# RWKV-7 chunks on one NeuronCore: the level products of two pairs of heads move to the crossed corners of the TensorE array, and the low-rank inputs of the factors are loaded a stage earlier

## The chip, the cores and the metric

The kernel runs on one core of one Trainium2 chip. The metric is the device time of one execution in microseconds (us), and less is better. A span or a start time in a profile counts from the first instruction of the profiled execution. TensorE is written PE, its weight loads PEld, VectorE DVE, ScalarE ACT, GpSimd POOL and SyncE SP.

## The reference, cut to what matters

One inference step of a hybrid layer: RWKV-7 time mixing and indexer-selected sparse attention side by side, merged by gates and followed by a gated convolutional FFN, for a prompt of 1024 + 16 tokens and 8 sample sequences of 8 tokens. Two parts of it matter here.

The first is how the RWKV inputs are prepared (`pm` holds the shifted projection, cut into r, k, v of 512 columns and three low-rank parts wd, ad, gd of 64, 64 and 128):

```python
w = -softplus(-(w0 + tanh(wd) @ w_w2)) - 0.5
decay = exp(-exp(w))
a = sigmoid(a0 + ad @ w_a2)
g = sigmoid(gd) @ w_g2
```

The second is the recurrence over tokens, for 8 heads with a 64 x 64 state each:

```python
def _rwkv7_step(S, inp):
    r, dec, k, v, kk, a = inp
    sa = einsum('bhvk,bhk->bhv', S, -kk)
    S = S * dec[..., None, :] + sa[..., None] * (kk * a)[..., None, :] + v[..., None] * k[..., None, :]
    return S, einsum('bhvk,bhk->bhv', S, r)
```

All values are fp32.

## The kernel before, in words

`program` runs stages one after another, each a block with a barrier behind it: normalisation and the attention projections, prompt attention with the remaining projections (`prompt_and_project`, it writes the 14 row tiles of the RWKV projection to `PM_dram`), the indexer scores of the samples (`sample_scores`, from L753), the RWKV factors (`rwkv_factors`, from L933), the RWKV chunks (`rwkv_chunks`, from L1136) and a `tail` with the rest. Every engine runs its own list in the order in which the code writes it; `wait_ge` on semaphores joins them. No planner reorders anything in these three stages.

**sample_scores.** POOL gathers 8 sequences of cached index keys into `KX` (L806, two buffers, the next gather waits until the buffer has been woven). ACT weaves two sequences into one tile (L818, semaphore `woven`), PE transposes them (L857), multiplies them with the queries (`dots`, L871), ACT rectifies (L830) and PE weighs them (L883). `dots` already uses four positions of the array: a product whose operands lie in partitions 0 to 63 or 64 to 127 writes its result to partitions 0 to 63 or 64 to 127, and all four combinations occur. Its moving operand is read with a step of 128 elements. SP writes scores to DRAM (L783 to L796) and waits for them at the end (L799).

**rwkv_factors.** SP issues 14 loads in this order: `PML` (the low-rank rows), `wa2` (two halves) and four vectors of `vec`, the k rows, two more parts of `vec`, then `g2`, `hsum`, `hback`, `keep`, `ones`, and last the r and v rows. ACT takes the tanh and the sigmoid of `PML` (L1037, L1038). PE and DVE wait for ten small loads (`small_in`, L990 and L1091) before they do anything. Then PE multiplies `PML` with `wa2` in 12 pieces (L997), ACT applies a sigmoid with a bias from `vec` (L1044), and DVE runs a scan with `keep` (L1098). ACT squares k (L1048), PE sums the squares (L1002), and 12 pieces of products and DVE work follow.

**rwkv_chunks.** 17 chunks of 64 tokens (the 17th with 16) and one chunk with the samples, 18 passes. Per chunk and head a unit lower triangular 64 x 64 matrix is inverted by levels of block doubling: 5 levels for a prompt chunk, 2 for the samples, 87 in all. Heads lie in pairs: pair p has one head in partitions 0 to 63 and one in 64 to 127. A level has these steps for all 8 heads:

- `level_q` on PE: Q = M Z into a PSUM bank A (8 matmuls, semaphore `q_done`), and right behind it the transpose of Z by a product with the identity into a bank B (8 matmuls, `t_done`).
- DVE masks Q out of bank A (L1503, `q_read`), and ACT copies the transpose out of bank B (L1432, `t_read`).
- `level_z` on PE: a product of the two into bank A (8 matmuls, `z_done`), and DVE adds it to Z (L1508, `z_ready`).

All three use `each`, whose matmuls have their operands and their result in the same half of the partitions:

```python
def each(out, lhsT, rhs, n=CH, at=0, step=CH):
    for p in range(4):
        for g in HEADS:
            o = at + step * p
            last = pe.matmul(out[g, o:o + n], lhsT(g, p), rhs(g, p), start=True, stop=True)
    return last
```

The order on PE is written out by hand. One pass c works on three chunks at once: the chain of chunk c (`chain_w`, `chain_u`, `chain_y`, `chain_s`, which carry the state), levels 2 to 4 of chunk c + 1, and the products (`gram_b`, `gram_t`, `gram_k`, `rows_bk`) and levels 0 and 1 of chunk c + 2. In full: chain_w(c), level_q(c+1, 2), gram_b, gram_t, chain_u, level_z(c+1, 2), gram_k, level_q(c+2, 0), chain_y, level_q(c+1, 3), chain_s, level_z(c+2, 0), level_z(c+1, 3), level_q(c+2, 1), level_q(c+1, 4), rows_bk, level_z(c+2, 1), level_z(c+1, 4). DVE does the two operations of the next state (L1514, L1516) between the mask of level 3 and the addition of level 0 of chunk c + 2. All matmuls of `each` are told apart in the profile by their tiles, not by their line: they are all L1233. An fp32 matmul stands in the trace as two records.

Of the kernel before, what the change touches and what calls it, by code (L numbers as in the profile page):

```python
# [4 lines left out]
F32 = mybir.dt.float32  # L5
I32 = mybir.dt.int32
U32 = mybir.dt.uint32
ALU = mybir.AluOpType
# [9 lines left out]
R = TP + TS  # L18
# [734 lines left out]
def sample_scores(nc, I, E, SC, ident):  # L753

    NR = 4 * 4
    with ExitStack() as sc:
        sc.enter_context(nc.cleanup_on_exit())
        def sb(name, shape, dt=F32):
# [14 lines left out]
                 "own_dotted", "own_rectified", "own_weighted", "own_placed", "own_sent")  # L773
        (woven, turned, evacuated, dotted, rectified, weighted, placed, ready,
         own_dotted, own_rectified, own_weighted, own_placed, own_sent) = (nc.alloc_semaphore(name=f"ss_{n}") for n in names)
        kx_in = [nc.alloc_semaphore(name=f"ss_kx_in{i}") for i in range(2)]
        sent = [nc.alloc_semaphore(name=f"ss_sent{i}") for i in range(2)]
        with nc.Block() as block:
            @block.sync
            def _(sp):  # L780
                sp.wait_ge(own_placed, 1)
# [30 lines left out]
            def _(act):  # L812
# [13 lines left out]
                for c in range(4 * NR):  # L826
# [4 lines left out]
                    if c % 16 == 7 and c // 16 < 2:  # L831
                        weave(c // 16 + 2)

# [98 lines left out]

def rwkv_factors(nc, I, PM_dram, PM, PML, F, PL):  # L933

    PARTS = [(0, 384), (384, 384), (768, 336)]
# [3 lines left out]
    with ExitStack() as sc:  # L939
# [3 lines left out]
        vec = sb("vec", [128, 7, 4])  # L943
        minus = sb("minus", [128, 4])
        wa2 = sb("wa2", [128, 512])
# [11 lines left out]
        names = ("small_in", "low_in", "k_in", "r_in", "v_in", "squashed", "squared", "sq_done", "bounded", "rooted",  # L957
                 "inverted", "w_done", "a_done", "g_done", "back_done", "bonus_done", "w_read", "a_read", "g_read",
                 "summed", "mapped", "normed", "bonused", "exps", "bonus_read")
        (small_in, low_in, k_in, r_in, v_in, squashed, squared, sq_done, bounded, rooted, inverted, w_done, a_done,  # L960
# [4 lines left out]
        with nc.Block() as block:  # L965
            @block.sync
            def _(sp):
                rows = PM_dram.rearrange("t p n -> p t n")
                sp.dma_start(PML[:, :, :], rows[:, 12:14]).then_inc(low_in, 16)
                for dst, src in ((wa2[0:64, :], I["w_w2"]), (wa2[64:128, :], I["w_a2"]),  # L970
                                 (vec[:, 0:4, :], I["rvec"][:, 0:4, :])):
                    sp.dma_start(dst, src).then_inc(small_in, 16)
                sp.dma_start(PM[:, 4:8], rows[:, 4:8]).then_inc(k_in, 16)
                for dst, src in ((vec[:, 5, :], I["rvec"][:, 4, :]), (vec[:, 6, :], I["lnb"]), (g2[:, :], I["w_g2"]),
                                 (hsum[:, :, :], I["hsum32"]), (hback[:, :, :], I["hback32"]),
                                 (keep[:, :], I["keep"]), (ones[:, :], I["ones_pair"])):
                    sp.dma_start(dst, src).then_inc(small_in, 16)
# [4 lines left out]
            def _(pe):  # L982
# [47 lines left out]
            def _(act):  # L1030
# [5 lines left out]
                act.wait_ge(low_in, 16)  # L1036
# [1554 lines left out]
```

## Time and profile before

| what | us |
|---|---|
| median of 3 timed runs (lowest, highest) | 3077.9 (3074.35, 3082.34) |
| the profiled execution's own time | 3106.72 |
| its span | 3104.9 |
| PE busy | 2777.5 (89%) |
| DVE busy | 1519.4 (49%) |
| ACT busy | 858.6 (28%) |

The three stages that the diff touches run one after another from 987 us of the span on. In a timeline a line holds the start, the length, the engine, the line of the code, the operation and its tiles, the number of records and, in brackets, the idle time ahead of it with what ended it. The times of matmuls in the trace overlap, because a matmul starts long before the one ahead of it has ended: a mean of 218 ns is the way of one through the array, and the distance between starts is what counts for throughput.

### The profile page before, as it was taken

Reading aid. Unit: us, or ns where it says so; the run is one execution under the profiler, and the core shown is the slowest. Engines: PE = TensorE matmul, PEld = TensorE weight load, DVE = VectorE, ACT = ScalarE, POOL = GpSimd, SP = SyncE. Lnnn points to the kernel's source line nnn. Section 1 sums busy time; section 2 is a strip of 40 time slices with the busy share of each in tenths; the row PEclk is TensorE's granted clock in tenths of the full one; section 3 lists DMA queues with packets and bytes.
Section 4 is the critical chain, followed back from the end, with each engine's and each line's share of the span. In section 5 each row is a group of like instructions: output and inputs, shape, how many; then the busy total and the mean of one; then the engine's idle time right before and its main releaser. Section 6 shows DMA issues by size and latency. Waiting matters only on the chain. (4 is left out here: it accounts for less than half of the span.)

```text
span 3104.9 us, 45137 instructions
## 1 busy us (share of the span) xinstructions
PE 2777.5 (89%) x17974; PEld 1725.7 (56%) x17974; DVE 1519.4 (49%) x2761; ACT 858.6 (28%) x1893; POOL 257.0 (8%) x291
## 2 busy tenths in 40 slices
PE   5897999998985968799869999979879999999998
PEld 3553466655653322799815566645546666556665
DVE  2001788894433426444356999998713320221111
ACT  1111522103533535222111233001235540134411
POOL 1000011000000000000000122000144410000000
PEclk9998999998996976899869999989889999999999
DMA  4001021231102440000016333225256643433332
GB/s 149 10 10 42 8 78 64 85 84 33 39 26 108 141 135 0 26 4 4 5 47 198 109 102 135 84 89 162 90 166 196 190 133 102 139 133 109 109 107 78
DMA packets 83041, 274.00 MB, mean 88 GB/s; under 512 B 17944, under 2 KB 39544, under 8 KB 70864
## 3 DMA queue, kind: packets, MB, share of 16 engines
q1 hardware_dynamic: 71056, 220.05, 21.6%
q0 software_dynamic: 11776, 51.07, 5.3%
q8 instruction: 142, 2.33, 0.3%
q14 instruction: 67, 0.55, 0.1%
HBM read 238.20 MB, written 32.16 MB: 87 GB/s over the span
## 5 line engine op out<-in xcount | busy, mean ns | idle before, releaser
L1885 PE MATMUL tl_P<-tl_XN,tl_WU 128*128 128x368 f32 x2112 | 670.9, 478 | 14.7 <-issue 8.6
L1885 PEld LDWEIGHTS tl_P<-tl_XN,tl_WU 128*128 128x128 f32 x2112 | 403.4, 192 | 269.5 <-issue 28.7
L346 PE MATMUL dp_PS<-xT,dp_W 128*128 128x368 f32 x1440 | 456.1, 474 | 0.0
L346 PEld LDWEIGHTS dp_PS<-xT,dp_W 128*128 128x128 f32 x1440 | 271.0, 191 | 163.0 <-issue 4.1
L1897 PE MATMUL tl_P<-tl_HT,tl_WD 128*128 128x368 f32 x1056 | 329.1, 473 | 0.0
L1897 PEld LDWEIGHTS tl_P<-tl_HT,tl_WD 128*128 128x128 f32 x1056 | 200.2, 190 | 125.6 <-issue 1.2
L625 DVE TENSOR_SCALAR_CACHE_REDUCE dp_EQ<-dp_SCORE,dp_trial 16x1040 f32<-16x1040 f32 (+6 forms) x217 | 215.7, 994 | 21.5 <-issue 0.9
L147 PE MATMUL pa_PG<-pa_W,xT 128*128 128x402 f32 (+1 forms) x576 | 204.0, 517 | 1.6 <-PEq L34 1.6
L147 PEld LDWEIGHTS pa_PG<-pa_W,xT 128*128 128x128 f32 (+1 forms) x576 | 110.8, 194 | 90.9 <-issue 21.0
L1847 PE MATMUL tl_P<-tl_Z 128*128 128x368 f32 x384 | 131.8, 508 | 32.9 <-DMA tl_Z<-in_wb 17.4
L2189 DVE MAX8 tl_v<-tl_Z 128x8 f32<-128x4100 f32 x32 | 141.8, 4432 | 3.5 <-issue 1.6
L2192 DVE FIND_INDEX8 tl_i<-tl_v,tl_Z 128x8 uint32<-128x4100 f32 x32 | 141.5, 4423 | 0.0
L2195 DVE MATCH_REPLACE8 tl_Z<-tl_v,tl_Z 128x4100 f32<-128x4100 f32 x32 | 141.2, 4414 | 0.3 <-issue 0.3
L2024 ACT ACTIVATE tl_SQ<-tl_X 128x368 f32<-128x368 f32 x44 | 22.4, 510 | 406.9 <-DVEq L2232 296.9
L2179 POOL DMA_INDIRECT tl_Z<-in_cache_kv,tl_PHT x128 | 123.2, 962 | 138.3 <-PE tl_P L1948 102.1
L1847 PEld LDWEIGHTS tl_P<-tl_Z 128*128 128x128 f32 x384 | 78.6, 206 | 86.8 <-DMA tl_Z<-in_wb 19.1
L1859 PE MATMUL tl_P<-tl_HT,tl_Z 128*128 128x368 f32 x384 | 120.1, 472 | 0.5 <-issue 0.5
L2060 ACT ACTIVATE tl_T<-tl_P,tl_cw 128x368 f32<-128x368 f32 (+1 forms) x66 | 42.3, 641 | 270.8 <-PE tl_P L1885 204.3
L187 DVE TENSOR_TENSOR pa_t<-pa_H,pa_cs 128x168 f32<-128x168 f32 (+1 forms) x9 | 3.0, 333 | 227.0 <-ACT pa_H L171 227.0
L2231 DVE TENSOR_TENSOR tl_X<-tl_X,tl_P 128x368 f32<-128x368 f32 x24 | 12.9, 538 | 180.0 <-PE tl_P L1897 179.4
L1859 PEld LDWEIGHTS tl_P<-tl_HT,tl_Z 128*128 128x128 f32 x384 | 72.9, 190 | 46.5 <-issue 1.0
L1998 DVE TENSOR_TENSOR tl_C<-tl_T 128x304 f32<-128x304 f32 x22 | 10.5, 475 | 171.0 <-ACTq L2072 171.0
(372 smaller groups left out, 3635.2 us busy)
## 6 DMA issues: line engine op xcount, KB each, us to landing
tl_WU<-in_wu SPq DMA_DIRECT2D x66, 1024.0 KB
tl_WD<-in_wd SPq DMA_DIRECT2D x48, 704.0 KB
dp_W<-in_w_rw SPq DMA_DIRECT2D x15, 1024.0 KB, 5.1
tl_Z<-in_wb SPq DMA_DIRECT2D x24, 512.0 KB, 3.8
tl_Z<-in_wo SPq DMA_DIRECT2D x24, 512.0 KB, 3.7
gates<-dp_PX SPq DMA_DIRECT2D x16, 552.0 KB, 3.6
tl_Z<-gates SPq DMA_DIRECT2D x48, 184.0 KB, 3.7
PM_dram<-dp_PMT SPq DMA_DIRECT2D x14, 552.0 KB, 2.7
```

Source lines behind the costliest of these rows:

```text
L147: last = pe.matmul(PG[0:n, c, 0:NC4], xT[:, k, r:r + n], W[:, k, NC4 * c:NC4 * c + NC4], start=k == 0, stop=k == KD - 1)
L346: last = pe.matmul(bank(f)[:, 0:w], W[:, t // 2 % 2, k, 128 * (t % 2):128 * (t % 2) + 128], xT[:, k, c:c + w], start=k == 0, stop=k == KD - 1)
L625: dve.tensor_scalar(EQ[0:n, 0:m], scored_of(j), values(n, x), None, op, ALU.add, accum_out=result[0:n, x:x + 1])
L1847: last = pe.matmul(out[:, 0:W], WM[:, i % 2, o:o + 128], YT[:, j, k, :], start=k == 0, stop=k == 3)
L1859: last = pe.matmul(out[:, 0:W], WM[:, i % 2, 128 * k:128 * k + 128], MT[:, k, :], start=k == 0, stop=k == KD - 1)
L1885: last = pe.matmul(out[:, 0:W], WU[:, i % 2, o:o + 128], XN[:, k, :], start=k == 0, stop=k == KD - 1)
L1897: last = pe.matmul(out[:, 0:W], WD[:, i % 3, 128 * e:128 * e + 128], HT[:, f, :], start=f == 0, stop=f == NF - 1)
L2060: act.activation(T[:, s, 0, 2:2 + w], pa[:, 0:w], ACT.Identity, bias=cb, scale=w0)
L2179: pool.indirect_dma_start(out=KV[:, n % 16, t, :], out_offset=None, in_=I["cache_kv"], in_offset=bass.IndirectOffsetOnAxis(ap=PHT[:, 64 * ...
L2189: dve.max(v8[:, :], SC)
L2192: dve.max_index(i8[:, :], v8[:, :], SC)
L2195: dve.match_replace(SC, v8[:, :], SC, TAKEN)
```

## The change

Low-rank inputs: `PML`, `wa2` and `vec` are allocated in `program` ahead of `sample_scores` and kept until the chunks are done. `sample_scores` loads them and applies the tanh and the sigmoid at the end of its ACT list. `rwkv_factors` issues the remaining small loads first, and its waits for them stand behind the first 12 products on PE, and ahead of the scans on DVE; ACT waits for none.

Level products: `corners` takes the place of `each` in the levels. Heads of pairs 0 and 1 write to their own half as before and to a first bank; heads of pairs 2 and 3 write to the other half and to a second bank. Q and the transposed Z then lie side by side in these two banks, crossed for pairs 2 and 3, and the product of the two (`home`) crosses back. The transposes come ahead of `q_done`, `t_done` is gone, and ACT's copy waits for `q_read`, since both now read the same banks.

```diff
 def sample_scores(nc, I, E, low, PM_dram, SC, ident):
             def _(sp):
+                for dst, src in ((low["wa2"][0:64, :], I["w_w2"]), (low["wa2"][64:128, :], I["w_a2"]),
+                                 (low["vec"][:, 0:4, :], I["rvec"][:, 0:4, :]), (low["vec"][:, 5, :], I["rvec"][:, 4, :]),
+                                 (low["vec"][:, 6, :], I["lnb"])):
+                    sp.dma_start(dst, src).then_inc(low_in, 16)
+                sp.wait_ge(woven, 4)
+                sp.dma_start(low["PML"][:, :, :], PM_dram.rearrange("t p n -> p t n")[:, 12:14]).then_inc(low_in, 16)
                 sp.wait_ge(own_placed, 1)
...
                         weave(c // 16 + 2)
+                act.wait_ge(low_in, 96)
+                act.activation(low["PML"][0:64, 0, :], low["PML"][0:64, 0, :], ACT.Tanh)
+                act.activation(low["PML"][:, 1, :], low["PML"][:, 1, :], ACT.Sigmoid)
...
 def rwkv_factors(nc, I, PM_dram, PM, low, F, PL):
             def _(sp):
-                sp.dma_start(PML[:, :, :], rows[:, 12:14]).then_inc(low_in, 16)
-                for dst, src in ((wa2[0:64, :], I["w_w2"]), (wa2[64:128, :], I["w_a2"]),
-                                 (vec[:, 0:4, :], I["rvec"][:, 0:4, :])):
+                for dst, src in ((keep[:, :], I["keep"]), (hsum[:, :, :], I["hsum32"]), (hback[:, :, :], I["hback32"]),
+                                 (g2[:, :], I["w_g2"]), (ones[:, :], I["ones_pair"])):
                     sp.dma_start(dst, src).then_inc(small_in, 16)
                 sp.dma_start(PM[:, 4:8], rows[:, 4:8]).then_inc(k_in, 16)
-                for dst, src in ((vec[:, 5, :], I["rvec"][:, 4, :]), (vec[:, 6, :], I["lnb"]), (g2[:, :], I["w_g2"]),
-                                 (hsum[:, :, :], I["hsum32"]), (hback[:, :, :], I["hback32"]),
-                                 (keep[:, :], I["keep"]), (ones[:, :], I["ones_pair"])):
-                    sp.dma_start(dst, src).then_inc(small_in, 16)
...
-                pe.wait_ge(small_in, 16 * 10)
-                pe.wait_ge(squashed, 1)
                 for u in range(NV):
...
                     pe.matmul(PW[u % 2][:, 0:w], wa2[0:64, 128 * c:128 * c + 128], PML[0:64, 0, cols], start=True,
                               stop=True).then_inc(w_done, 1)
+                pe.wait_ge(small_in, 16 * 5)
...
-                act.wait_ge(low_in, 16)
-                act.activation(PML[0:64, 0, :], PML[0:64, 0, :], ACT.Tanh)
-                act.activation(PML[:, 1, :], PML[:, 1, :], ACT.Sigmoid)
-                act.drain().then_inc(squashed, 1)
-                act.wait_ge(small_in, 16 * 10)
...
-                dve.wait_ge(small_in, 16 * 10)
                 dve.tensor_scalar(vec[:, 4, :], vec[:, 3, :], -1.0, 1.0, ALU.mult, ALU.add)
                 dve.tensor_scalar(minus[:, :], vec[:, 2, :], -1.0, None, ALU.mult)
                 dve.drain()
+                dve.wait_ge(small_in, 16 * 5)
...
 def rwkv_chunks(nc, I, PM, F, PL, s_out, ss_out, yr_dram, ident):
-        A0, A1, B0, B1, G0, G1, C0, C1 = (
-            sc.enter_context(nc.psum_tensor(f"rc_P{i}", [128, 512], F32)) for i in range(8))
+        LV = sc.enter_context(nc.psum_tensor("rc_LV", [128, 2, 2, 512], F32))
+        square_of = lambda s: LV[:, s, :, 0:2 * CH].rearrange("p b (e n) -> p b e n", e=2)
+        turned_of = lambda s: LV[:, s, :, 2 * CH:4 * CH].rearrange("p b (e n) -> p b e n", e=2)
...
+                def corners(s, at, lhsT, rhs, home):
+                    for e in range(2):
+                        for b in range(2):
+                            p = 2 * b + e
+                            for g in range(2):
+                                held, out = HEADS[g], HEADS[g ^ b]
+                                if home:
+                                    held, out = out, held
+                                o = at + CH * e
+                                last = pe.matmul(LV[out, s, b, o:o + CH], lhsT(held, p), rhs(held, p), start=True, stop=True)
+                    return last
...
-                    each(AA[s], lambda g, p: MV[g, n % 3, p, 0:CH], z).then_inc(q_done[s], 1)
-                    each(BB[s], z, eye).then_inc(t_done[s], 1)
+                    corners(s, 0, lambda g, p: MV[g, n % 3, p, 0:CH], z, False)
+                    corners(s, 2 * CH, z, eye, False).then_inc(q_done[s], 1)
...
-                    each(AA[s], lambda g, p: ZT2[g, s, p, :], lambda g, p: Q2[g, s, p, :]).then_inc(z_done[s], 1)
+                    corners(s, 0, lambda g, p: ZT2[g, s, p, :], lambda g, p: Q2[g, s, p, :], True).then_inc(z_done[s], 1)
...
-                    act.wait_ge(t_done[s], before(n) + l + 1)
-                    act.activation(ZT2[:, s], half(BB[s]), ACT.Copy).then_inc(t_read[s], 1)
+                    act.wait_ge(q_read[s], before(n) + l + 1)
+                    act.activation(in_banks(ZT2[:, s]), turned_of(s), ACT.Copy).then_inc(t_read[s], 1)
...
-                    dve.tensor_tensor(Q2[:, s], half(AA[s]), one(MQ + l), ALU.mult).then_inc(q_read[s], 1)
+                    dve.tensor_tensor(in_banks(Q2[:, s]), square_of(s), mask, ALU.mult).then_inc(q_read[s], 1)
...
-                    dve.tensor_tensor(Z2[:, n % 3], Z2[:, n % 3], half(AA[s]), ALU.add).then_inc(z_ready[s], 1)
+                    dve.tensor_tensor(z, z, square_of(s), ALU.add).then_inc(z_ready[s], 1)
```

## Rows read from the trace of the kernel before

**Rows 1.** Windows: length, then busy us and (instructions) per engine, PE clock, DMA.

```profile
1132.60:1148.80 16.20, 0.00 (x0) 0.00 (x0) 0.01 (x1) 3.53 (x3) 0.00 (x0) 0.50 0.96 331
1257.60:1279.70 22.10, 20.34 (x529) 19.86 (x531) 9.95 (x21) 3.89 (x9) 0.00 (x0) 0.88 0.10 40
1279.70:1522.80 243.10, 232.94 (x7429) 230.74 (x7426) 116.74 (x257) 58.73 (x144) 0.00 (x0) 1.00 0.02 4
```

**Rows 2.** Waits in the chunks, PE alone: us in total, times, longest.

```profile
PE rc_P L1233 <- DVE rc_Z L1508: 11.2, 18, 0.6
```

**Rows 3.** Timeline of PE: first records of passes 0 and 16, and level_q in pass 3.

```profile
1279.68 0.22 PE L1287 MATMUL rc_P<-rc_ST,PM 64*64 64x64 f32 x1
...
1326.23 0.63 PE L1233 MATMUL rc_P<-rc_Z,rc_MV 64*64 64x64 f32 x16
1326.69 0.63 PE L1233 MATMUL rc_P<-rc_masks,rc_Z 64*64 64x64 f32 x16
...
1522.86 0.23 PE L1287 MATMUL rc_P<-rc_ST,rc_XP 64*64 64x64 f32 x2
```

**Rows 4.** Timeline of all engines around the stall of one pass.

```profile
1319.66 0.28 PE L1345 MATMUL rc_P<-rc_U,rc_BK 64*64 64x64 f32 x4
1319.99 0.42 DVE L1514 TENSOR_TENSOR rc_ST<-rc_ST,rc_P 128x256 f32<-128x256 f32 x1 [0.98 <-PE rc_P L1345]
1321.51 0.68 PE L1233 MATMUL rc_P<-rc_Z,rc_MV 64*64 64x64 f32 x16 [0.63 <-DVE rc_Z L1508]
...
1323.17 0.42 DVE L1503 TENSOR_TENSOR rc_Q<-rc_P,rc_masks 128x256 f32<-128x256 f32 x1 [0.51 <-PE rc_P L1233]
...
1323.64 0.38 ACT L1432 ACTIVATE rc_ZT<-rc_P 128x256 f32<-128x256 f32 x1 [0.55 <-PE rc_P L1233]
```

**Rows 5.** Timeline of PE, products at several positions of the array.

```profile
721.48 1.12 PE L434 MATMUL dp_PS<-dp_PTS,V 128*64 128x32 f32 x31
...
989.11 0.30 PE L846 MATMUL ss_PW<-ss_RLQ,ss_WB 128*32 128x8 f32 x8 [0.86 <-DVEq L920]
...
1040.48 1.93 PE L871 MATMUL ss_PS<-ss_KT,QB 64*64 64x512 f32 x8 [1.41 <-ACT ss_RL L830]
...
1123.73 1.06 PE L883 MATMUL ss_PW<-ss_RL,ss_WB 128*32 128x512 f32 x8 [1.20 <-ACT ss_RL L830]
...
1529.38 1.05 PE L1300 MATMUL rc_P<-PM,rc_SS 64*64 64x8 f32 x32
```

**Rows 6.** Waits from 1124 to 1149 us: us in total, times, longest.

```profile
PE rf_P L997 <- DMA rf_ones<-in_ones_pair: 24.0, 1, 24.0
```

**Rows 7.** Timeline of SP, ACT and PE from the samples' end into the factors.

```profile
1122.59 1.09 ACT L830 ACTIVATE ss_RL<-ss_PS 128x512 f32<-128x512 f32 x2 [1.77 <-PE ss_PS L871]
...
1132.62 0.39 SPq L969 DMA_DIRECT2D PML<-PM_dram  x1
...
1139.72 1.28 ACT L1038 ACT_TABLE_LOAD   x1
1141.01 1.12 ACT L1038 ACTIVATE PML<-PML 128x1104 f32<-128x1104 f32 x1
...
1148.81 15.09 PE L997 MATMUL rf_P<-PML,rf_wa 64*128 64x384 f32 x24 [24.01 <-DMA rf_ones<-in_ones_pair]
```

**Rows 8.** DMA issues from 1132 us: count, KB each, median us to landing.

```profile
PM<-PM_dram SPq DMA_DIRECT2D x3, 2208.0 KB, 14.4
PML<-PM_dram SPq DMA_DIRECT2D x1, 1104.0 KB, 6.0
rf_keep<-in_keep SPq DMA_DIRECT2D x1, 552.0 KB
```

**Rows 9.** DMA rate from 985 to 1035 us, 1.25 us a slice; ACT's third weave.

```profile
GB/s 52 0 7 157 210 419 446 433 420 420 419 419 13 197 210 419 406 419 406 406 419 433 26 197 288 419 433 354 197 288 419 419 328 39 0 0 0 0 0 0
...
1032.33 7.13 ACT L818 ACTIVATE ss_KXI<-ss_KX 128x4096 f32<-128x4096 f32 x2
```

**Rows 10.** Window of the prompt attention with gaps on PE.

```profile
880.00:905.00 25.00, 19.56 (x104) 12.09 (x105) 7.81 (x27) 9.37 (x20) 0.00 (x0) 1.00 0.04 14
```

More of the change, by code:

```diff
@@ L750, with sample_scores @@
 HALF = (PAST + QS) // 2
-def sample_scores(nc, I, E, SC, ident):
+def sample_scores(nc, I, E, low, PM_dram, SC, ident):
     NR = 4 * 4
@@ L930, in _, with rwkv_factors @@
                 place(NR - 1)
-def rwkv_factors(nc, I, PM_dram, PM, PML, F, PL):
+def rwkv_factors(nc, I, PM_dram, PM, low, F, PL):
+    PML, wa2, vec = low["PML"], low["wa2"], low["vec"]
     PARTS = [(0, 384), (384, 384), (768, 336)]
@@ L1158, in rwkv_chunks @@
         YN = sb("YN", [128, 2, 368])
[L1159 to L1161 removed]
+        LV = sc.enter_context(nc.psum_tensor("rc_LV", [128, 2, 2, 512], F32))
+        G0, G1, C0, C1 = (sc.enter_context(nc.psum_tensor(f"rc_P{i}", [128, 512], F32)) for i in range(4))
+        A0, A1, B0, B1 = LV[:, 0, 0], LV[:, 1, 0], LV[:, 0, 1], LV[:, 1, 1]
+        square_of = lambda s: LV[:, s, :, 0:2 * CH].rearrange("p b (e n) -> p b e n", e=2)
+        turned_of = lambda s: LV[:, s, :, 2 * CH:4 * CH].rearrange("p b (e n) -> p b e n", e=2)
+        in_banks = lambda t: t.rearrange("p (b e) n -> p b e n", b=2)
         names = ("small_in", "started", "padded", "gram", "g_dve", "g_act", "w1_done", "w1_read", "wt_read", "u_done",
@@ L1502, in level_q @@
                     dve.wait_ge(q_done[s], before(n) + l + 1)
-                    dve.tensor_tensor(Q2[:, s], half(AA[s]), one(MQ + l), ALU.mult).then_inc(q_read[s], 1)
+                    mask = masks[:, MQ + l:MQ + l + 1, :].rearrange("p (a b) n -> p a b n", a=1).to_broadcast([128, 2, 2, CH])
+                    dve.tensor_tensor(in_banks(Q2[:, s]), square_of(s), mask, ALU.mult).then_inc(q_read[s], 1)
                 def level_z(n, l):
@@ L2446, in program, with sr @@
                 prompt_and_project(nc, I, S, E, T, xT, ya_dram, PM_dram, O["shift"], gates, ident)
-            sample_scores(nc, I, E, SC, ident)
-        with ExitStack() as hold:
-            def sr(name, shape):
-                return hold.enter_context(nc.sbuf_tensor(name, shape, F32))
-            early = sr("early", [128, 3 * 4 * R])
-            F = {n: early[:, 4 * R * i:4 * R * i + 4 * R].rearrange("p (c r) -> p c r", c=4)
-                 for i, n in enumerate(("B", "G", "RKK"))}
-            PM = sr("PM", [128, 16, R])
-            F["A"] = PM[:, 12:16]
-            PL = sr("PL", [128, 4, 25])
-            with ExitStack() as lowrank:
-                PML = lowrank.enter_context(nc.sbuf_tensor("PML", [128, 2, R], F32))
-                rwkv_factors(nc, I, PM_dram, PM, PML, F, PL)
-            rwkv_chunks(nc, I, PM, F, PL, O["state_p"], O["state_s"], yr_dram, ident)
+            low = {"PML": se("PML", [128, 2, R]), "wa2": se("wa2", [128, 512]), "vec": se("vec", [128, 7, 4])}
+            sample_scores(nc, I, E, low, PM_dram, SC, ident)
+            with ExitStack() as hold:
+                def sr(name, shape):
+                    return hold.enter_context(nc.sbuf_tensor(name, shape, F32))
+                early = sr("early", [128, 3 * 4 * R])
+                F = {n: early[:, 4 * R * i:4 * R * i + 4 * R].rearrange("p (c r) -> p c r", c=4)
+                     for i, n in enumerate(("B", "G", "RKK"))}
+                PM = sr("PM", [128, 16, R])
+                F["A"] = PM[:, 12:16]
+                PL = sr("PL", [128, 4, 25])
+                rwkv_factors(nc, I, PM_dram, PM, low, F, PL)
+                rwkv_chunks(nc, I, PM, F, PL, O["state_p"], O["state_s"], yr_dram, ident)
         tail(nc, I, S, SC, gates, yr_dram, ya_dram, O["v"], O["conv"], O["y"], ident)
```

17 lines of the change are left out of this document (8 added, 9 removed).

## The prediction

> **What bounds the kernel now.** I read the windows of the stages first, then the waits, then the timeline of one pass.
>
> In the chunks PE is the bound. From the first record of pass 0 to that of pass 16 PE is busy 232.9 of 243.1 us, at a granted clock of 1.00, the 2.4 GHz level, while DVE is busy 117 us and ACT 59 us [rows 1]. The two first records stand 1522.86 - 1279.68 = 243.18 us apart, so a pass takes 15.20 us [rows 3]. PE waits for one thing in them, 18 times: for DVE's update of Z ahead of level 1, 0.6 us each [rows 2]. The reader is to see two things in the timeline: the distance between two groups of eight level matmuls, 1326.69 - 1326.23 = 0.465 us (to the third digit it is 16 records by 29 ns), while a group is shown 0.63 us long, so that the way through the array is 0.63 - 0.465 = 0.16 us [rows 3].
>
> The second place is the start of the factors. From 1132.6 to 1148.8 us PE does nothing at all [rows 1]. The wait that ends last there is for `ones`, the tenth small load [rows 6]; it was issued behind the first low-rank rows and the k rows, 1.1 and 2.2 MB [rows 8]. The first product starts at 1148.81 us and the stage's first load is issued at 1132.62 us, 16.2 us earlier [rows 7].
>
> **Level products on four corners.** Removed from PE: nothing in count, 24 matmuls (48 records) a level stay. What changes is how many run at once. Two heads of a pair sit on two positions of the array that share neither rows nor columns; 16 records take 0.465 us, 58 ns for every two. With four positions in turn, 16 records would be four rounds and not eight: 4 x 58 = 0.233 us. Per level, three groups: 3 x 0.233 = 0.70 us less. A pass has 5 levels: 3.50 us.
>
> Does a round of four last as long as a round of two? The trace has no such round with 64 columns, so I bound it. From below: four positions that share all rows and split the columns. Eight records of 512 columns take 1.06 us at L883 [rows 5], and with 0.16 for the way through that is two rounds of 0.45 us; eight one after another would take as long as two rounds four times over. Here four moving streams enter the same rows at full rate. Weights: two positions over the same rows at L434, whose moving side is only 32 columns, come at (1.12 - 0.16) / 15.5 = 62 ns for two; two on separate rows and columns at L1300, with 8 moving columns, at (1.05 - 0.16) / 16 = 56 ns [rows 5]. So a load of 64 weight columns is what sets the 56 to 62 ns, and sharing rows adds at most 6. Records can also leave fast enough: eight at L846 take 0.30 us in all, 0.14 without the way through, under 20 ns each, where a round of four needs 58 / 4 = 15 ns [rows 5]; that is the tighter point. From above: L871, which does use the four crossed positions, needs 1.93 us for eight records of 512 columns [rows 5]. That is (1.93 - 0.16) / 2 = 0.89 us a round of four, or just what four rounds of two at 0.44 us would give. So the one crossed product in the trace runs no faster than two positions would. Its moving operand is read with a step of 128 elements, the one of L883 is not, and the level products are not. The bounds are thus 58 ns (gain as above; a gain beyond it is excluded, since each position by itself needs that long) and 116 ns (no gain). I take 58, since every pair of positions by itself (same rows, L434 and L883; neither, L1300) shows it, and the step is the one thing that L871 has alone.
>
> The Trainium skill says, in SBUF — State Buffer, section "Door 1: The DMA port swizzle", that reads which leave a 16-byte line each time pay a penalty; by it L871 is slow for its step, and the sum stays as it is. The trace shows nothing against that.
>
> **The waits that this opens.** Q and the transpose now signal together, after two short groups of 0.233 us each, which is 0.465 us after the first starts: DVE can mask at the time at which it could before. ACT's copy then waits for DVE: before, DVE starts at 1323.17 and ACT at 1323.64, 0.47 us later [rows 4], which is one group; after, it is one DVE operation of 0.42 us and some 0.08 us for the semaphore, 0.50 us. So a level's latency stays, while PE has less to do meanwhile. I walked the written order once with these lengths (chain_w 0.94, chain_y 1.40, the two 128-column products 0.88 each, everything else with 16 matmuls 0.94 and with 8 0.465; the levels as above). The same walk with the lengths of before gives 15.20 us a pass, as measured. After, PE starts chain_s at 7.13 us of the pass and leaves it at 8.07. From the end of chain_s (its last four records start at 1319.66, four take 0.12) to level_q(c+2, 1) the trace has 1321.51 - 1319.78 = 1.73 us [rows 4]: DVE's two state operations stand ahead of the Z update there. Before, two level_z filled 0.93 us of it and PE stood 0.80 (0.63 of that is shown idle, since the last matmuls are still on their way); after, they fill 0.47, and PE stands some 1.25. Two other copies arrive 0.03 us late each (level_z(c+1, 3) and (c+1, 4)); they are the next to be late if a copy were slower. All other waits have over 0.3 us of room. The pass: 10.84 us of PE work (14.34 - 3.50) + 1.25 + 0.06 = 12.15, and 12.19 in the walk, which also gives 15.20 and not 14.34 + 0.80 for before: -3.01 us. Sixteen passes: -48.2 us. Ahead of pass 0 stand 7 levels, 7 x 0.70 = 4.9 us of PE work, but few other products to fill the latency; the walk gives -2.9 us there (in that stretch PE was busy 20.3 of 22.1 us [rows 1]). Chunks: **-51.1 us**. The last pass and what follows it have no level: 0.
>
> DVE's and ACT's operations keep their 256 elements a partition, now in two banks. The trace has no operation over two banks. From below 0; from above I take what the wide and narrow masks leave open, 0.08 us an operation, which in the walk costs 4.6 us in all. I take 0.
>
> **Low-rank inputs.** In the factors PE, ACT and DVE have nothing to wait for at the stage's start, so the first product moves from 1148.81 to about 1132.7: -16.1 us. Will the rest follow? The 12 products and sigmoids are 15.1 us long as before [rows 7], at the same 1.2 GHz level (0.50 [rows 1]). The scans need `keep`: SP issues five loads of together 1.13 MB (`keep` is half [rows 8]), at 420 GB/s [rows 9] 2.7 us plus some 2.5 of issue: there at 1139 us. The scans then run without gaps and end with the sigmoids. The k rows, 2.2 MB, 5.4 us later, are there by 1145, and the squares start at 1148.4; r (1150) and v (1156) are wanted after 1170. **-16.1 us**; if the k rows took the 14.4 us to landing of before [rows 8] from an issue at 1135, squares would start 1 us late.
>
> In the samples' stage SP gets six loads. Five, 0.27 MB, compete with the first gather: 0.27 / 0.42 = 0.6 us at most, and in the slices at 157 and 210 GB/s there is room [rows 9]; I take **+0.5**. SP's own score writes now stand behind `woven` 4; they move from 990 to 1019 us, nobody waits for them before the stage's end. `PML`, 1.1 MB, goes beside the fifth and sixth gather. DMA is done by about 1026 us there, 2.7 us more make 1029, and ACT weaves at 1032.3 without a gap [rows 9]: 0, or 3 us if the gathers slip. The tanh and the sigmoid, 1.12 + 1.28 + 1.12 = 3.5 us, follow the last Relu at 1123.7 and end at 1127.3, while the next stage starts at 1132.6 [rows 7] because of the last score writes: covered by 5 us.
>
> Sum: -51.1 - 16.1 + 0.5 = **-66.7 us**. The profiled execution took 3106.72 us and would take 3040.0. The median of the timed runs is 28.8 us lower; I take the same difference off it: 3077.9 - 66.7 = **3011 us**.
>
> **Rivals.** (A) *The four corners share something, and a round of four takes 116 ns.* For it: L871 above. Against: L434 and L883. The chunks then gain nothing; the fused signal costs 1.2 us ahead of pass 0. 3077.9 - 15.6 + 1.2 = 3063.5 us. The Trainium skill has a rule of this kind: in TensorE: Matmul & The Clock Gate, section "Part 3: Packing small matmuls — row/col tiling", weight loads overlap matmuls under way only when the row group differs; crossed positions share row groups, so by it a round would take two weight loads, and the time would be this rival's. The 62 ns of L434, whose positions share all rows, speak against the rule here. (B) *Issue bound*: a record every 22 ns, about the 0.14 us for seven steps of L846, 20 ns. A round of four takes 87 ns, half the gain: the walk gives 13.68 us a pass, -25.4 us, 3037 us. (C) *Not faster: the clock.* PE's idle share of a pass grows from 4% to 1.31 / 12.19 = 11%, in one gap of 1.2 us. If the granted clock fell to 0.50 in the loop, PE's 10.84 us would become 21.7. Against it: in the prompt attention PE is busy only 19.6 of 25 us with the clock at 1.00 [rows 10]. The point from which it decides: the other gains are 3.01 us a pass and 15.6 once, together some 3.9 us a pass of 17, against 10.8 us for a pass wholly at the low level, so it is slower than before if the low level holds over 37% of the loop. With half of it: 5.4 - 3.0 = 2.4, by 17 is +41, -15.6: 3103 us. (D) The low-rank part alone fails, since a load is late: 3011 + 10 = 3021, inside the main range.
>
> **How the numbers follow.** Main case 0.77, its own range 3000 to 3026 (one side the spread of the timed runs and 4 us that the clock's phases in the stages behind can give, the other side 4.6 for two banks, 3 for the gathers and 4). A 0.12, B 0.07, C 0.04. The range that holds the time 8 times in 10 reaches to B: 2998 to 3038. A measurement tells about 0.3%, 9 us, from no change; A is at -0.47%, near enough that a third of it may come out as the same. Faster 0.92, same 0.04, slower 0.04.
>
> **What would show it.** A pass of 12.2 us between first records of chain_w; 16 level records starting in 0.233 us, the third and fourth some 13 and 20 ns behind the first; one wait of PE for DVE's Z update of 1.1 to 1.25 us a pass; ACT's copy 0.5 us behind DVE's mask; clock 1.00 from pass 0 to 16. In the factors the first product within 0.3 us of the stage's start, and the stage 16 us shorter. Wrong if the groups still stand 0.465 us apart (A), at 0.35 (B), if the clock shows 0.50 in the loop (C), or if ACT's weaves wait longer for gathers.

## The result, and the profile after

The change makes the kernel faster, by about half of what was forecast. Median 3042.5 us (3040.2 to 3044.6, four runs) against 3078.5 us (3074.4 to 3082.3, four runs) of before; ratio 0.9883, 95% interval 0.9866 to 0.99. Forecast were 3011 us and a range of 2998 to 3038. The profiled execution of after took 3044.58 us (span 3042.8). That of before was 28.8 us over its median and this one is 2.1 over its own, so from trace to trace only the stages that the change touches are compared.

| place | before, us | after, us | difference | forecast |
|---|---|---|---|---|
| last Relu of the samples | 1123.68 | 1119.43 | -4.25: -3.79 from the stages ahead, -0.46 in this one | +0.5 in this one |
| first low-rank product | 1148.81 | 1128.41 | -16.15 beyond that | -16.1 |
| first record of pass 0 | 1279.68 | 1257.31 | -2.0 beyond that | -2.9 |
| first record of pass 16 | 1522.86 | 1483.09 | -17.4 beyond that | -48.2 |

The samples' stage itself took 134.94 us from its first activation to its last Relu, where it was 135.40 us, so the forecast's +0.5 does not show in it.

The factors first. The timeline of after, as [rows 7] for before (start, us, engine, line, what, [idle before <- releaser]):

```profile
1118.34 1.09 ACT L837 ACTIVATE ss_RL<-ss_PS 128x512 f32<-128x512 f32 x2 [1.77 <-PE ss_PS L881]
1119.31 1.11 ACT L841 ACTIVATE PML<-PML 64x1104 f32<-64x1104 f32 x1
...
1121.72 1.12 ACT L842 ACTIVATE PML<-PML 128x1104 f32<-128x1104 f32 x1
...
1128.37 0.35 SPq L980 DMA_DIRECT2D rf_keep<-in_keep  x1
...
1128.41 15.06 PE L999 MATMUL rf_P<-PML,wa 64*128 64x384 f32 x24 [7.87 <-PEq L756]
```

The tanh and the sigmoid follow the last Relu and are done at 1122.84, 5.5 us before the next stage. The first product stands 0.04 us behind the stage's first load, where 16.2 us lay between them.

The chunks. Windows, as [rows 1]: first the stretch ahead of pass 0, then passes 0 to 15:

```profile
1237.10:1257.30 20.20, 17.30 (x528) 16.23 (x530) 9.80 (x21) 3.67 (x9) 0.00 (x0) 0.80 0.09 35
1257.30:1483.10 225.80, 193.59 (x7440) 184.64 (x7434) 115.47 (x256) 58.43 (x145) 0.00 (x0) 0.99 0.02 4
```

PE is busy 193.6 us, 39.3 less than before, but the stretch is only 17.3 shorter: a pass takes (1483.09 - 1257.31) / 16 = 14.11 us and PE now stands still 32 of 226 us. What for? Timeline of PE in pass 6, with the level groups that answer to [rows 3] on top:

```profile
1347.41 0.46 PE L1246 MATMUL rc_LV<-rc_Z,rc_MV 64*64 64x64 f32 x16
1347.66 0.44 PE L1246 MATMUL rc_LV<-rc_masks,rc_Z 64*64 64x64 f32 x16
1347.89 0.31 PE L1333 MATMUL rc_P<-rc_RN,rc_MV 64*64 64x64 f32 x4
...
1350.11 0.28 PE L1358 MATMUL rc_P<-rc_U,rc_BK 64*64 64x64 f32 x3
1351.51 0.27 PE L1358 MATMUL rc_P<-rc_U,rc_BK 64*64 64x64 f32 x1 [1.12 <-issue]
1351.51 0.38 PE L1356 MATMUL rc_P<-rc_MV,rc_BK 64*64 64x64 f32 x4
```

Two groups of 16 level records start 0.24 us apart, where it was 0.465: the four corners do run at once, a round of four takes what a round of two took. But in the middle of chain_s, between two records of one product group that wait for no semaphore, PE stands 1.12 us with the releaser "issue". The largest waits of PE in passes 0 to 15 (us in total, times, longest) say how often:

```profile
PE rc_LV L1246 <- DVE rc_Z L1523: 11.5, 12, 1.1
PE rc_LV L1246 <- issue: 9.9, 20, 0.9
PE rc_P L1234 <- issue: 3.9, 9, 0.6
PE rc_P L1358 <- issue: 3.5, 4, 1.1
```

Before, the wait for Z was PE's only row in these passes; the "issue" rows are new:

```profile
PE rc_P L1233 <- DVE rc_Z L1508: 10.2, 16, 0.6
```

Measured from start to start they are 48 stalls of over 0.15 us, together 31.1 us, 1.9 us a pass. That is as much as the distance of 14.11 from the forecast's 12.19, but in part by chance: the waits for Z came to 0.88 us a pass (12 of them, 14.1 us from start to start) and not to 1.25, and what is left of a pass is 11.3 us and not 10.9. Where do the stalls stand? At no particular product, but at every 254th record. Windows from the end of one stall to the end of the next:

```profile
1324.32:1327.91 3.59, 2.98 (x127) 2.75 (x128) 1.96 (x5) 1.36 (x3) 0.00 (x0) 1.00 0.02 5
1327.91:1331.97 4.06, 3.71 (x127) 3.58 (x127) 2.10 (x5) 0.77 (x2) 0.00 (x0) 1.00 0.01 4
1331.97:1335.88 3.91, 3.60 (x127) 3.52 (x127) 1.90 (x4) 1.10 (x3) 0.00 (x0) 1.00 0.03 6
1367.63:1371.19 3.56, 2.90 (x127) 2.62 (x127) 2.09 (x5) 1.36 (x3) 0.00 (x0) 1.00 0.02 5
```

Each window holds 127 matmuls and 127 weight loads (in the first, one more that reaches in over its edge), and two or three waits that are instructions of their own and that the views do not count: 256 instructions. With these waits counted from the trace, the 48 stalls lie whole multiples of 256 instructions apart; outside that grid the trace has 8 more gaps of this size that no semaphore ends, 1.7 us in all. The view of DMA queues over passes 0 to 15 has a queue for them, of 16 KB packets (0.95 MB / 58), 64 bytes an instruction:

```profile
q8 instruction: 58, 0.95, 1.7%
```

The mean distance between the starts of the 58 packets is 3.86 us. Such a packet starts 1.28 us behind the end of a stall (median), is under way for 1.05 us (mean), and a stall ends 1.38 us behind a landing (median). That last figure is the closest link between the two: all 48 stalls end 1.20 to 1.61 us behind the landing of a packet, while the waits for Z end anywhere between 0.63 us ahead of one and 2.07 us behind. So one block of 256 instructions is fetched while the one before it is executed, no sooner, and a block that PE would get through in less than some 3.7 us waits for the next.

Before, a block took 15.20 x 256 / 937 = 4.15 us of PE's time on average (a pass has 928 records and 9 waits that are instructions), single blocks 3.68 to 4.58 us, and there was no stall in 243 us. Its packets, on the same queue:

```profile
q8 instruction: 59, 0.97, 1.7%
```

### The profile page after: what moved, and what is told of

It reads as the page before. It is cut to its first block and busy times, and to the rows that moved or that the text cites. A ratio compares the mean times of both kernels' runs of the same rounds, so it can differ in the third digit from the quotient of the medians.

```text
span 3042.8 us, 45136 instructions
## 1 busy us (share of the span) xinstructions
PE 2723.9 (90%) x17974; PEld 1674.2 (55%) x17974; DVE 1517.8 (50%) x2761; ACT 857.7 (28%) x1893; POOL 257.6 (8%) x291
## 3 DMA queue, kind: packets, MB, share of 16 engines
q8 instruction: 142, 2.33, 0.3%
## 5 line engine op out<-in xcount | busy, mean ns | idle before, releaser
L1900 PEld LDWEIGHTS tl_P<-tl_XN,tl_WU 128*128 128x128 f32 x2112 | 403.1, 192 | 258.5 <-issue 17.4
L1862 PE MATMUL tl_P<-tl_Z 128*128 128x368 f32 x384 | 131.9, 508 | 32.7 <-DMA tl_Z<-in_wb 17.6
L2246 DVE TENSOR_TENSOR tl_X<-tl_X,tl_P 128x368 f32<-128x368 f32 x24 | 12.9, 538 | 180.0 <-PE tl_P L1912 179.4
```

The source lines that it names most:

```text
L1862: last = pe.matmul(out[:, 0:W], WM[:, i % 2, o:o + 128], YT[:, j, k, :], start=k == 0, stop=k == 3)
L1900: last = pe.matmul(out[:, 0:W], WU[:, i % 2, o:o + 128], XN[:, k, :], start=k == 0, stop=k == KD - 1)
```

## The experiments

Theory F is the account just given: PE's instructions arrive in blocks of 256, one each 3.7 to 3.9 us, and where PE wants them faster, it waits at the border of a block. Its rivals: P, PE's own work is longer than the rounds say; D, the round trips through VectorE and ScalarE hold the passes; L, the low-rank part gives little by itself; M, the two parts disturb each other. The runs were made in three sets, each beside runs of before on its chip (medians 3076.5 us for 1, 2, 3 and the wide transposes of 6, 3078.3 for after again, padded after and 7, 3099.7 for 4, padded before and 8); each ratio is against before in its set.

**1. The low-rank part alone** (chunks as before).

> The low-rank part alone: tanh, sigmoid, PML, vec and wa2 in the samples' stage, the chunks as in the kernel before. Forecast's step: -16.1 us, so about 3062 us; passes of 15.20 us as before, no stalls of PE without a releaser. Theory (F: the missing 29 us of the sum are lost in the chunks, because PE's instructions arrive in blocks of 256, one each 3.86 us, and the chunks' matmuls now want them faster): this part is worth its full 16.1 us. Rival (L: the low-rank part itself gives little of its gain to the end, the rest was noise of the profiled executions): under 8 us, 3070 us or more.

Measured: 3062.0 us, ratio 0.995 (0.9937 to 0.9963), -14.5 us. In its trace the passes take 15.20 us, with no "issue" row. L is out, and -16.1 was right within the interval (-11 to -19).

**2. The corners alone** (factors and samples' stage as before).

> The crossed corners alone, factors and samples' stage as before. Forecast's step: -51.1 us, 3027 us. Theory F: 937 instructions a pass at 15.06 ns each (3.86 us for 256) make a pass of 14.1 us instead of 15.20, so 17 us over 16 passes and 2 ahead of them: about 3059 us, with a stall of 0.3 to 1.3 us on PE after each 254 records. Rival (M: the two parts disturb each other, in memory or in the order of the code, and each alone gives what was forecast): 3027 us and passes of 12.2 us. Rival (D: the passes are held by the round trips through DVE and ACT): also about 3059, but the stalls then stand at the waits for q_read and z_ready and not at each 254th record.

Measured: 3048.0 us, ratio 0.9912 (0.9899 to 0.9925), -28.5 us. M is out: the corners alone do not give what was forecast either. The passes take 13.55 us in its trace and the stalls are there, 38 of them, 22.6 us from start to start, again whole multiples of 256 instructions apart (6 other gaps take 1.3 us), as F has it and D not. The expectation was 9 to 11 us too pessimistic, because the time from block to block was 3.70 us there and not 3.86. The two parts alone add to -43.0 us, together they gave -36 to -37.7. The intervals of the three ratios (4 to 5 us to either side each) are wide enough for this difference; whether there is one stays open.

**3. After without the levels' transposes.** ScalarE copies Z itself, so the result is not the reference's.

```
-  corners(s, 0, ..MV.., z, False)
-  corners(s, 2 * CH, z, eye, False).then_inc(q_done[s], 1)
+  corners(s, 0, ..MV.., z, False).then_inc(q_done[s], 1)
-  act.activation(in_banks(ZT2[:, s]), turned_of(s), ACT.Copy)
+  act.activation(ZT2[:, s], Z2[:, n % 3], ACT.Copy)
```

> The kernel after without the transposes of the levels: ScalarE copies Z itself to ZT2, so the result is not the reference's. It takes 32 instructions from each level, 160 of 937 from a pass; the round trip from square to product keeps its three steps. Theory F: a pass is 777 instructions at 15.06 ns = 11.7 us, 2.4 us less, over 16 passes and the start some 40 us: about 3002 us, and stalls each 254 records are there still. Rival P (PE's own work, the rounds of four, is the pass): 5 x 0.23 us less, so 12.95 us a pass and 3023 us. Rival D (round trips through DVE and ACT): the transposes lie beside the mask of the square, nothing is gained: 3040 us.

Measured: 3005.3 us, ratio 0.9772 (0.9758 to 0.9786), some 34 us under after by the ratios; 11.84 us a pass. F said 11.7, P 12.95, D no gain. The trace has 49 packets, again one each 3.89 us, though PE's work had become shorter by 1.17 us a pass. P and D are out as the bound of after.

That 11.84 is so close to 11.7 is partly luck. The blocks hold this kernel only in part: 23 stalls at multiples of 256 instructions take 10.0 us from start to start, the 16 waits for Z take 18.2, and the two last passes, which have no such stall, take 11.23 us.

```profile
PE rc_LV L1246 <- DVE rc_Z L1522: 14.7, 16, 1.1
```

**4. Before without the levels' transposes**, the same cut where blocks don't bind. Here too the result is not the reference's.

> The kernel before without the transposes of the levels (ScalarE copies Z itself, the result is not the reference's). The old level's transposes are 8 rounds of 58 ns, 0.466 us, so PE's work falls by 2.33 us a pass. Theory F: here a pass of 777 instructions needs 11.7 us of blocks and PE's work, 12.87 us, binds: 17 x 2.33 = 40 us less, 3038 us, with few or no stalls at block borders. The same cut in the kernel after gave 35 us though it takes only half as much PE work there (1.17 us a pass), which the work alone does not explain. If this one gains clearly less than 35 us, the round trips (D) bind in both.

Measured: ratio 0.9878 (0.9863 to 0.9893), -38.6 us, passes of (1475.6 - 1269.8) / 16 = 12.87 us. The windows and the only wait of PE in them:

```profile
1269.80:1475.60 205.80, 195.59 (x6150) 193.40 (x6146) 116.77 (x257) 61.31 (x144) 0.00 (x0) 1.00 0.02 4
```

```profile
PE rc_P L1233 <- DVE rc_Z L1507: 10.2, 16, 0.6
```

No "issue" row: 777 instructions in 12.87 us are 4.24 us a block. The same 160 instructions less are worth 2.3 us a pass in both kernels, in before for the work they are (2.33), in after for the blocks they fill (0.625 of a block).

**5. After again, after with 88 idle instructions a pass, and before with the same.** Of four waits written in a row, two stand in the trace as instructions of their own. The padded after has the same four lines in `corners` too.

```
 for p in range(4):
+    for _ in range(4 if p % 2 == 0 else 0):
+        pe.wait_ge(started, 1)
```

> The kernel after, unchanged, on the chip and in the hour of the runs beside it, since the corners alone had passes of 13.55 us against 14.11 here. If the mean time from one block of PE's instructions to the next (3.86 us in the trace of after, 3.70 in that of the corners) belongs to the chip or the hour, the passes come out near 13.5 us and the whole near 3033; if it belongs to the program, 14.1 us and 3042.

> The kernel after with 88 more instructions on PE in each pass that do no work (waits on a semaphore that has long been raised, two at each of 44 places between the products), 1025 instead of 937. Theory F (a block of 256 instructions each 3.86 us): a pass becomes 4.0 blocks, 15.4 us, 1.3 more: about 3064 us, and 23 fewer matmul and weight records between two stalls. Rival P (PE's matmuls set the pass; a wait that is already met costs nothing): 14.1 us, 3042. Rival D (round trips): 3042 too.

> The kernel before with the same 88 waits a pass (two at each of 44 places) that the padded kernel after has; there they cost 3.9 us a pass where theory F gave 1.3, and the trace shows each such wait some 0.05 us long on PE's weight side. This prices the waits themselves where the blocks do not bind: a pass of 15.20 us plus their own cost. If they cost 3.9 us here too, 3144 us, the padded kernel after says nothing for or against F by its time, only by where its stalls stand. If they cost 2.5 us or less (3121 or less), the rest in the padded kernel after is the blocks' (theory F). If they cost nothing, 3078, all of it is.

After again: 3040.6 us, ratio 0.9878 (0.9862 to 0.9895), 13.84 us a pass. The mean block was 3.78 us, between 3.70 and 3.86, so it varies with the execution; the whole time does not follow it closely.

Padded after: 3106.3 us, ratio 1.0097 (1.0081 to 1.0114), +66 us, 3.9 a pass. Padded before: ratio 1.0162 (1.0146 to 1.0178), +49 us, 2.9 a pass. By the threshold set beforehand (2.5 or less) the two times decide nothing, and my price of 1.3 us was wrong. The traces tell the parts. In padded before, 49 stalls at block borders take 27.1 us from start to start, 1.7 us a pass; the waits for Z are 0.4 us a pass shorter, so that some 1.5 us a pass are the waits' own. In padded after, the stalls at borders grew from 25.0 us to 44.4 (1.2 us a pass), the waits for Z nearly vanished (0.9 us a pass less), and some 3.6 us a pass are the waits' own. What decides is where the stalls stand. Windows of padded after, from stall to stall:

```profile
1322.42:1327.30 4.88, 3.90 (x113) 3.50 (x114) 1.95 (x5) 0.77 (x2) 0.00 (x0) 1.00 0.02 3
1327.30:1332.24 4.94, 4.13 (x117) 3.67 (x116) 1.96 (x4) 1.37 (x3) 0.00 (x0) 1.00 0.01 3
1332.24:1337.18 4.94, 3.98 (x113) 3.78 (x113) 2.56 (x5) 0.77 (x2) 0.00 (x0) 1.00 0.02 3
1337.18:1341.17 3.99, 3.20 (x121) 3.10 (x122) 1.27 (x3) 0.77 (x2) 0.00 (x0) 1.00 0.02 4
```

227, 233, 226 and 243 records (the second window takes in two over its edge, it is 231), and with the 29, 25, 30 and 13 wait instructions that the trace has there, 256 each time. The border counts instructions of any kind, not matmuls. And padded before, which has no crossed corners, now has the same kind of stall, which before has not:

```profile
PE rc_P L1235 <- issue: 16.7, 31, 1.0
```

So the corners do not cause the stalls, the stream of instructions does. Here the packets start later behind the border (2.1 us in the median against 1.28) and a block takes 4.4 to 4.5 us; "3.86 us a block" is thus no constant. What in a block triggers the fetch of the next is open.

**6. Fewer instructions for the same result.** The transposes of a level become two of 128x128, 4 instructions for 32; since those swap a head's half with its place, the square goes crosswise and comes back (cut to what matters; VectorE adds Z in the matching order):

```
+ for q in range(2):
+   for j in range(2):
+     for g in range(2):   # head (g, 2q+j): rows of half g, out to half j in bank g
+       corner(s, q, j, g, MV[HEADS[g], n % 3, 2*q+j, 0:CH], Z2[HEADS[g], n % 3, 2*q+j, :])
+ for q in range(2):
+   last = pe.transpose(LV[:, s, q, 2*CH:4*CH],
+             Z2[:, n % 3, 2*q:2*q+2, :].rearrange("p a n -> p (a n)"), ident[:, :])
  ...
+ last = corner(s, q, g, j, ZT2[HEADS[j], s, 2*q+g, :], Q2[HEADS[j], s, 2*g+q, :])
```

> Candidate with fewer instructions: the transposes of a level as two PE transposes of 128x128 (two heads of a half and both halves at once, 4 instructions instead of 32); the square of head (g, 2q+j) goes to half j in bank g, the product with the turned Z comes back to half g. A pass has 797 instructions instead of 937. Theory F: the blocks allow a pass of 12.0 us; the two changes of tile shape a level (about 0.16 us each, from other changes of shape before) and the two wide transposes against eight small ones put 0.2 us on each level, a pass of 13.2 to 13.5 us if nothing else binds: 3028 to 3032 us in all, faster than the kernel after by 10 to 14. Rival D or P (waits or PE's work bind and not the instructions): 0.2 us more on each of five levels, slower than after by 17: 3059 us.

Measured: 3030.1 us, ratio 0.9848 (0.9835 to 0.9861), 11 us under after by the ratios, though its PE is busy longer (200.2 us in 217.8 against 193.6 in 225.8):

```profile
1257.10:1474.90 217.80, 200.21 (x6309) 179.10 (x6309) 113.62 (x255) 58.27 (x144) 0.00 (x0) 1.00 0.02 4
```

```profile
PE rc_LV L1276 <- DVE rc_Z L1535: 17.6, 16, 1.1
PEld rc_P L1234 <- issue: 5.4, 32, 0.2
PEld rc_LV L1276 <- issue: 3.1, 17, 0.4
```

Passes of 13.61 us, each like the next, 4.37 us a block. That is 0.1 us above the 13.2 to 13.5 us expected. The stalls at borders are gone; what is left as "issue" is 0.2 us on the weight side each time a 64x64 group follows the 128x128 transposes. The Trainium skill, TensorEngine Tiling (Array Packing), section "Key Properties", has that a change of tiling mode drains TensorE. The idle 0.2 us agree with that, though the trace shows them on the way back from 128x128 only.

**7. The wait for Z made shorter, in both.** Two kernels, the kernel after and the one of experiment 6, with one edit on VectorE:

```
-  if chain: next_state(c)
   if new: level_z(n, 0)
   if ahead: level_z(x, 3)
+  if chain: next_state(c)
```

> The kernel after with VectorE's two updates of the state put behind the Z updates of the levels n,0 and x,3 instead of ahead of them: the wait of 1.1 to 1.3 us that PE has once a pass for rc_Z shrinks by what two such updates take until then, some 0.65 us. Theory F: most of that is only time in which the next block of instructions comes in; at most 3 us in all: 3039 to 3042. Rival D (round trips): 17 x 0.65 us = 11 less, 3031.

> The same move of the state's updates in the candidate with the wide transposes, whose trace shows no stalls at block borders and a wait for rc_Z of 1.32 us in each pass. Theory F: here the wait is on the path, 17 x 0.65 us = 11 less than the candidate's 3030: 3019. If the move gives nothing here either, then it is the wait that was not shortened, and the two runs say nothing on F.

Measured: after with it 3040.0 us against 3040.6 without: nothing. With fewer instructions 3019.9 us, ratio 0.9814 (0.9796 to 0.9832), against 3030.1: -10. The largest waits of the first,

```profile
PE rc_LV L1246 <- issue: 9.9, 21, 0.8
PE rc_P L1234 <- issue: 7.6, 12, 1.0
PE rc_LV L1246 <- DVE rc_Z L1523: 2.3, 8, 0.3
```

and of the second:

```profile
PE rc_LV L1276 <- DVE rc_Z L1535: 5.2, 16, 0.3
```

In both the wait was shortened (from 12.9 us in after again and 17.6 us in all). In the kernel after the same time came back as stalls at the borders: from start to start the waits for Z and for ScalarE's copy fell from 16.2 us in after again to 6.5, and the border stalls rose from 25.0 to 34.9. Where the blocks do not bind, the pass fell from 13.61 to 12.84 us. This is the clearest separation of F from D, and the second kernel is the best one found: 58 us under before where after is 37.

**8. The rest of the wait filled.** Eight transposes of BE moved ahead of level_q(n, 1).

> The candidate with the wide transposes and the early Z updates, with the eight transposes of BE (0.47 us of PE's work) moved from behind level_q(x, 4) to ahead of level_q(n, 1), where the trace shows PE waiting 0.7 us a pass for rc_Z. What they covered behind level_q(x, 4), the copy of the turned Z on ScalarE, is then covered 0.2 us less. So 0.2 to 0.3 us less a pass: 3.5 to 5 us under the 3019.9 of that candidate, about 3016 us. If the blocks bind again (797 instructions, 12.0 us a pass at 3.86 us a block, against 12.84 now), nothing: 3020.

Measured: ratio 0.9815 (0.9801 to 0.9828), the same as without (0.9814). The wait is gone from the trace, but the mean pass is 12.88 us against 12.84. Three passes are longer than the rest, 13.1, 13.0 and 13.9 us, and the longest has a stall of 0.97 us at a block border, so 797 instructions a pass are near where blocks bind once more. That is not the main reason: the undisturbed passes take 12.75 us against 12.81, only 0.06 less. The sixteen passes without the edit and with it:

```profile
1260.10:1465.60 205.50, 200.28 (x6309) 179.18 (x6310) 111.77 (x256) 58.30 (x144) 0.00 (x0) 1.00 0.02 4
1259.15:1465.28 206.13, 204.95 (x6320) 183.34 (x6313) 112.99 (x257) 56.89 (x145) 0.00 (x0) 1.00 0.02 4
```

PE is now busy 99% of the time. The wait was filled, and PE's busy time grew by nearly as much; why the same instructions keep it busy 4.7 us longer in this order is not shown.

## Why the prediction was wrong

*The low-rank part* held: -16.15 us by the trace, -14.5 by its own timed run, with the activations hidden. The weave behind the first gather starts 0.8 us later, counted from the stage's first activation, and that is made up by the last Relu.

*A round of four takes 58 ns*: right. Groups stand 0.24 us apart. So rival A was wrong, and so is for this case the rule of the Trainium skill that the prediction set beside it (TensorE: Matmul & The Clock Gate, section "Part 3: Packing small matmuls — row/col tiling"): the four corners share row groups and still load weights under one another's matmuls, four loads each 58 ns while each matmul is shown 218 ns long. The strided operand as the reason for L871's slowness was not tested.

*The waits that this opens*: right in place, and in size where no stall stands beside them. The forecast had one wait for Z a pass, 1.1 to 1.25 us; the trace has it in 12 of 16 passes, and the longest is 1.1 us of shown idle and 1.31 from start to start. ScalarE's copy was to start 0.5 us behind VectorE's mask: 1348.68 against 1348.24 us, 0.44.

*The pass*: this is the step that failed. "10.84 us of PE work + 1.25 + 0.06 = 12.15, and 12.19 in the walk" takes each instruction to be at hand when its operands are; the sum has no term for the supply of instructions. The term -48.2 us measured -17.4. Experiments 3, 4 and 7 show what stood in its place: PE's 937 instructions a pass come in blocks of 256, 3.66 a pass, at 3.70 to 3.86 us each, so 13.5 to 14.1 us. Shrinking PE's work below some 15 ns an instruction bought nothing, and neither did a shorter wait. Ahead of pass 0, -2.0 us against -2.9, it was something else: no stall like these stands there, but a stretch at the low clock that before has not (below, under rival C).

*Rival B, issue bound*, had nearly the right time (3037) by the wrong mechanism; that is luck. It looked at the spacing of neighbouring records, which within a round of four is 6 to 9 ns, so nothing binds there. The rate that mattered is that of 256 instructions together, and it stood in the trace of before: 59 instruction packets, one each 4.16 us on average, beside no stall. The forecast read DMA there only as a share of 0.02 [rows 1]. The bound should have been asked for: the forecast wanted a block each 12.19 x 256 / 937 = 3.33 us, while the mean in this stage was 4.16 and the shortest single distance 3.44. But no row of before gives the bound itself. Its packets started only 0.0 to 0.9 us behind the border and landed 1.8 to 3.5 us ahead of the next, so that the supply looked faster there than it proved to be once PE caught up with it; why they start 1.0 us or more behind a border at which PE has stalled is open.

The Trainium skill, Runtime: NRT & Kernel Launch, section "Instruction fetch mechanics", says that an engine's instructions are refilled in blocks of 16 KiB, 256 instructions, the next while the current one is executed. The trace agrees with both. The section also says that this is hidden, since dispatch is slower than the refill. Here it is not, with up to 1.34 us from start to start at a border.

*Rival C, the clock*: in the profiled execution the grant was 0.50, the 1.2 GHz level, for one stretch of 3.4 us, from 1354.3 us on. It lies behind the stall and the wait of pass 6, 1.34 and 1.31 us from start to start with 1 us of work between them; that pass took 15.8 us. Elsewhere in the loop the grant stayed at 1.00, also behind a pair of 1.31 and 1.32 us in pass 12:

```profile
1354.30:1357.70 3.40, 3.40 (x112) 3.40 (x102) 0.93 (x3) 1.31 (x3) 0.00 (x0) 0.50 0.02 5
1437.70:1441.10 3.40, 3.40 (x159) 3.40 (x161) 1.84 (x5) 1.36 (x3) 0.00 (x0) 1.00 0.02 5
```

Half of the 3.4 us is an estimate of the price, 1.7 us in all: not the mechanism of the loop. Ahead of pass 0 it weighs more. There the low level came back for another 3.4 us, behind a stretch in which PE was busy half of the time, while before the grant stayed at 1.00 from 1262.76 us on:

```profile
1241.64:1245.05 3.41, 1.71 (x76) 1.46 (x75) 1.44 (x3) 0.38 (x1) 0.00 (x0) 1.00 0.00 0
1245.05:1248.47 3.42, 2.87 (x80) 2.68 (x75) 0.85 (x2) 0.98 (x2) 0.00 (x0) 0.50 0.02 5
1262.76:1279.70 16.94, 15.22 (x469) 14.73 (x467) 8.14 (x18) 3.89 (x9) 0.00 (x0) 1.00 0.01 3
```

The last line is of before. Half of the 2.87 us in which PE was busy at the low level, 1.4 us, is an estimate of the price, and more than the 0.9 us that are missing there.

*The sum*: -16.1, -51.1 and +0.5 were forecast, -66.7; by the traces it is -16.15, -1.97 and -17.40, together -35.5, and by the medians -36.0.

## What to carry to other kernels

Count TensorE's instructions per stage (an fp32 product is two matmuls and two weight loads) together with the waits that stand as instructions, and divide the stage's time by them. In this kernel the supply of instructions held the stage where it wanted less than some 15 ns an instruction, or 3.7 to 3.9 us for 256, and with many waits in between already at 4.5 us; kernels at 4.1 to 4.4 us for 256 ran with hardly a stall. Where a change would get a stage below that, fewer, larger instructions can help and shorter ones do not. Such a bound shows as "issue" stalls at a fixed count of instructions, wherever in the code that is, beside 16 KB packets on an instruction queue. A saving that moves a wait on an engine bound in this way is worth trying again once the count is down: here one edit was worth nothing before and 10 us after.

## What the runs showed of the hardware that was not expected

- PE's next 256 instructions are fetched as one 16 KB packet of about 1.05 us. Behind a border at which PE has stalled it starts 1.0 us or more later (up to 3.0 us with many waits), and over the 307 border stalls of seven traces PE goes on 1.18 to 1.61 us behind its landing. The mean time from block to block there is 3.70 to 3.89 us with plain matmuls, 4.4 to 4.5 with many waits between them.
- Semaphore waits that are already met are not free between small matmuls: 88 instructions of them cost the kernel before 2.9 us a pass, 33 ns each with the border stalls that they bring, by estimate some 18 ns each without.
- Four crossed 64x64 positions take 16 records in 0.24 us.
- Going back from 128x128 to 64x64 tiles leaves the weight side idle for 0.2 us.
- A stall of 1.34 us and a wait of 1.31 us, 1 us of work apart, were followed by the 1.2 GHz level; a pair of 1.31 and 1.32 us in another pass of the same trace was not. What decides is open.
